# The turns of two score steps in one run of every second slot

## The chip, the cores and the metric

The kernel runs on one core of one Trainium2 chip. The metric is the device time of one launch in microseconds (us). The kernel before takes 1454.48 us (median of three runs, 1454.06 to 1455.24). Engines are named as in the profile: PE is TensorE (its weight loads are PEld), DVE is VectorE, ACT is ScalarE, POOL is GpSimd, SP issues the weight loads from memory.

## What is computed

Two residual layers over x (512 tokens, width 1024). Each layer normalises x, projects it by `w_in`, runs two attention mixers of 16 heads of 64 columns over the 512 tokens, gates, projects, merges and adds. What matters here are the mixers. The sparse one (NSA) has two softmax branches per head over full causal keys (the selection takes all eight blocks, the window is as long as the sequence) and a small compressed branch with 31 keys; the other (FoX) has one causal softmax per head with a forgetting bias:

```python
s = jnp.einsum('bqhd,bkhd->bhqk', qc, k).astype(jnp.float32) * scale
s = s + Fq[..., None] - F[:, :, None, :]
p = masked_softmax(s, mask)
return jnp.einsum('bhqk,bkhd->bqhd', p.astype(v.dtype), v)
```

So per layer there are 16 x 3 causal attentions of 512 x 512, each in four query tiles of 128 rows, whose key widths are 128, 256, 384 and 512.

## The kernel before

Every matmul is done in two parts for precision: an fp32 operand is split into an upper part (rounded, by ACT) and a lower part (the rest, by DVE).

A layer's attentions run in eight **cycles** (function `cycles`), one per pair of heads, each followed on all engines by a `body(cycle)` of its own. A cycle has 24 **steps**: 16 for NSA (two heads, two branches, four query tiles, in the order of `NSA_ORDER`, whose widths are 256, 128, 128, 384, 512, 256, 384, 512 columns, twice) and 8 for FoX (128, 256, 384, 512, twice). The first and the last cycle of a layer have variants; the six between are alike, and are called steady below.

A step passes through the engines:

1. PE makes its scores (`score_step`, L1874 and L1876), in two PSUM banks;
2. DVE takes the row maximum and copies the scores out (`max_step`, L1400, with a read of the accumulator);
3. ACT exponentiates and sums (`exp_step`, L936, with a read of the accumulator);
4. DVE inverts the sum (`invert_step`, L1407), POOL scales the row (`scale_step`, L727 and L730);
5. PE turns the probabilities, one transpose per 128 columns, into one of two PSUM banks (`turn_step`, L1889);
6. ACT copies out the upper part (`hi_step`, L945), then DVE the lower part (`lo_step`, L1412), into a buffer for an attention of that parity;
7. when an attention's four steps are done, PE multiplies with the values (`value_step` L1914, and the last key tile later, `value_narrow` L1922), into one bank, `o_pair`. After a head's last attention ACT copies that bank's lower half (`lower_half`, L950) and DVE adds the upper half (`head_output`, L1419).

The work is written out as **slots**, and the order in a slot is the order in which an engine's queue has it. In slot s of a cycle:

- PE: turns of step s-2 (LAG_TURN = 2), scores of step s+1, then a piece of the projections of the next pair (`unit_piece`, L1814), then what is in `extra` (values of a step s-4 that ends an attention, the compressed branch). The turn of step n waits until the lower part of step n-2 is out of its bank.
- ACT: exponent of step s, upper part of step s-2, then its list `todo` (splits of weights `w_hi` L807, roundings of q, k and v, `lower_half`).
- DVE: reciprocal of step s-1, maximum of step s, lower part of step s-3 (LAG_PT = 3, `lo_step` waits for that step's upper part), then its `todo` (`w_lo` L1217, copies of the projections, `head_output`).
- POOL: scaling of step s-1, then its `todo`.

How many of the 144 unit matmuls of a cycle stand in a slot is set by `Plan`: it gives each slot the costs of scores, turns and values (`busy`) and spreads the units over what is left (`spread`). The slots in which a unit begins and ends (`plan.begin`, `plan.end`) place the splits and copies on ACT and DVE.

Of the kernel before, what the change touches and what calls it, by code (L numbers as in the profile page):

```python
# [51 lines left out]
CYCLE_STEPS = 24  # L52
# [5 lines left out]

GAINS, PLACES = (DEPTH + 1) * KT, 2 * DEPTH * CJ
LAG_SCALE, LAG_TURN, LAG_PT, LAG_PV = 1, 2, 3, 4  # L60
PT_COLS = 3 * 384 + T


# [10 lines left out]
    return cum  # L74


NSA_ORDER = [(0, 1), (0, 0), (1, 0), (0, 2), (0, 3), (1, 1), (1, 2), (1, 3)]
SCORE_COST = {(0, 0): 1.0, (1, 0): 0.0}


class Plan:


    def __init__(self, last=False):
        self.last = last
        self.slots = CYCLE_STEPS + (LAG_PV if last else 0)
        busy = [0.0] * self.slots
        for s in range(self.slots):
            for lag, cost in ((-1, self.score_cost), (LAG_TURN, self.turn_cost), (LAG_PV, self.value_cost)):
                if not last or s - lag < CYCLE_STEPS:  # L90
                    busy[s] += cost((s - lag) % CYCLE_STEPS)
        for s, cost in ((1, 2.0), (5, 2.0), (9, 1.0), (17, 1.0)):
            busy[s] += cost
        self.cum = spread(24 * 6, busy)
        self.begin, self.end = {}, []
        for u in range(6):
            first = next(s for s in range(self.slots) if self.cum[s] > 24 * u)
            self.begin.setdefault(first, []).append(u)
            self.end.append(next(s for s in range(self.slots) if self.cum[s] >= 24 * u + 24))
# [88 lines left out]
def bass_trunk(nc, x, norm_g, w_in, b_forget, pe_k, w1_k, w2_k, pe_v, w1_v, w2_v, w_nsa, w_fox,  # L188
               w_out, final_g, rope_c, rope_s, out):
    ctx = ExitStack()  # L190
    with ctx:
# [429 lines left out]
        def _(pool):  # L621
# [66 lines left out]
            def gate_output(pair):  # L688

                pool.wait_ge(o_read, 2 * pair.r + 3)  # L690
                apart(pool)
                pool.wait_ge(z_done, pair.r + 2)
                apart(pool)
                y = y_all[0 if pair.nsa else 1][:, bass.ds(pair.i, 1), :]
                pool.tensor_tensor(y, y, z_silu[:, pair.b:pair.b + 1, :], ALU.mult).then_inc(y_mul, 1)
# [37 lines left out]
            def body(cycle):  # L733
                plan, l, i = cycle.plan, cycle.l, cycle.i
                todo = {}

                def at(slot, what):
                    todo.setdefault(slot, []).append(what)

                at(0, lambda: bias_of(cycle.fox))  # L740
                at(2, lambda: compressed_shift(cycle.nsa.m))
                at(4, lambda: compressed_scale(cycle.nsa.m, i))
                if not cycle.first:
                    at(10, lambda: gate_output(Pair(False, l, i - 1, cycle.g)))
                at(CYCLE_STEPS + 1 if cycle.last else 16 + LAG_PV + 2, lambda: gate_output(cycle.nsa))
                if cycle.last:
                    at(CYCLE_STEPS + LAG_PV, lambda: gate_output(cycle.fox))
                else:
                    at(plan.end[2] + 4, lambda: q_sin(l * 10 + 3 + i))
                    at(plan.end[2] + 5, lambda: q_sum(l * 10 + 3 + i))  # L750
                for s in range(max([plan.slots] + [k + 1 for k in todo])):
                    if s < plan.slots and s - LAG_SCALE < CYCLE_STEPS and cycle.step(s - LAG_SCALE):
                        scale_step(*cycle.step(s - LAG_SCALE))
                    for what in todo.get(s, []):
                        what()
# [43 lines left out]
        def _(act):  # L799
# [100 lines left out]
            def body(cycle):  # L900
# [3 lines left out]
                def at(slot, what):  # L904
                    todo.setdefault(slot, []).append(what)
# [34 lines left out]
                def hi_step(pair, s):  # L940
                    a, qt = pair.at(s)
                    act.wait_ge(s_turned, pair.s0 + s + 1)
                    if pair.starts(s) and not (cycle.first and pair.nsa and a < 2):
                        act.wait_ge(pv_mm, pair.a0 + a - 1)
                    act.activation(pt_tiles(pt_hi, a, qt), turned_tiles(s, qt), ACT.Copy)\  # L945
                        .then_inc(pt_hi_done, 1)

                def lower_half(pair, h):
                    act.wait_ge(pv_mm, pair.a0 + pair.steps // QT // 2 * (h + 1))
                    act.activation(o_low[:, h, :], o_pair[HD:2 * HD, :], ACT.Copy, scale=0.5).then_inc(o_low_done, 1)  # L950

                if not cycle.first:
                    before = Pair(False, l, i - 1, cycle.g)
                    at(0, lambda: lower_half(before, 0))
                    at(LAG_PV, lambda: lower_half(before, 1))
                at(8 + LAG_PV, lambda: lower_half(nsa, 0))
                at(16 + LAG_PV, lambda: lower_half(nsa, 1))
                if cycle.last:
                    at(CYCLE_STEPS, lambda: lower_half(fox, 0))
                    at(CYCLE_STEPS + LAG_PV, lambda: lower_half(fox, 1))  # L960
                    at(plan.end[4] + 3, lambda: gate_tanh(l, 0, 0))

# [18 lines left out]
                for s in range(max([plan.slots] + [k + 1 for k in todo])):  # L981
                    if s < CYCLE_STEPS:
                        exp_step(*cycle.step(s))
                    if s < plan.slots and s - LAG_TURN < CYCLE_STEPS and cycle.step(s - LAG_TURN):
                        hi_step(*cycle.step(s - LAG_TURN))
                    for what in todo.get(s, []):
                        what()

# [224 lines left out]
        def _(dve):  # L1213
# [130 lines left out]
            def body(cycle):  # L1344
# [76 lines left out]

                if not cycle.first:
                    before = Pair(False, l, i - 1, cycle.g)
                    at(1, lambda: head_output(before, 0))
                    at(LAG_PV + 2, lambda: head_output(before, 1))
                at(8 + LAG_PV + 2, lambda: head_output(nsa, 0))
                at(16 + LAG_PV + 1, lambda: head_output(nsa, 1))
                if cycle.last:
                    at(CYCLE_STEPS + 1, lambda: head_output(fox, 0))
                    at(CYCLE_STEPS + LAG_PV, lambda: head_output(fox, 1))  # L1430

                m = nsa.m
# [348 lines left out]
        def _(pe):  # L1781
# [58 lines left out]
            def body(cycle):  # L1840
                plan, l, i, nsa, fox = cycle.plan, cycle.l, cycle.i, cycle.nsa, cycle.fox
                extra = {}
# [104 lines left out]
                        pe.wait_ge(cmp_pt_lo, nsa.m + 1)  # L1947
                    pe.matmul(o_pair[:, :], vcb[:, nsa.g, h, :], pc_t[:, :], start=False, stop=False)  # L1948

                for slot, what in ((1, cmp_scores), (5, cmp_turn), (9, lambda: cmp_values(0)),  # L1950
                                   (17, lambda: cmp_values(1))):
                    extra.setdefault(slot, []).insert(0, what)
                for s in range(plan.slots):

                    now = cycle.step(s - LAG_PV)
                    if s - LAG_PV < CYCLE_STEPS and now and now[0].ends(now[1]):
                        extra.setdefault(s, []).append(lambda now=now: value_step(now[0], now[0].at(now[1])[0]))

                def ended_at(s):

                    now = cycle.step(s - 1 - LAG_PV) if s - 1 - LAG_PV < CYCLE_STEPS else None
                    return (now[0], now[0].at(now[1])[0]) if now and now[0].ends(now[1]) else None

                if cycle.first:
                    score_step(nsa, 0)
# [2 lines left out]
                for s in range(max([plan.slots] + [k + 1 for k in extra])):  # L1968
                    scored = cycle.step(s + 1) if s < CYCLE_STEPS else None
                    narrow = scored and not scored[0].nsa and scored[0].starts(scored[1])  # L1970
                    if s < plan.slots and s - LAG_TURN < CYCLE_STEPS and cycle.step(s - LAG_TURN):
                        turn_step(*cycle.step(s - LAG_TURN), scored=scored if narrow else None, ended=ended_at(s))
                    elif s < plan.slots and ended_at(s):
                        value_narrow(*ended_at(s), 0)
                        value_narrow(*ended_at(s), 1)
                    if scored and not narrow:
                        score_step(*scored)
                    want = plan.cum[s] if s < plan.slots else done
                    while done < want:
                        u = done // 24  # L1980
                        stop = min(want, 24 * u + 24)
                        unit_piece(done - 24 * u, stop - 24 * u, *cycle.unit(u), free=bank_read(cycle, u))
                        done = stop
                    for what in extra.get(s, []):
                        what()
                if cycle.last:
                    value_narrow(*ended_at(plan.slots), 0)
                    value_narrow(*ended_at(plan.slots), 1)

            def run_in(n):  # L1990
                for _ in range(n):
# [232 lines left out]
```

## Time and profile before

| | |
|---|---|
| Time, median of three runs | 1454.48 us |
| Span of the profiled execution | 1452.2 us |
| PE busy | 1443.0 us (99%) |
| DVE busy | 1050.6 us (72%) |
| ACT busy | 915.4 us (63%) |
| POOL busy | 469.1 us (32%) |
| Chain that ended last | PE 98%, DVE 1% |
| Most of the chain | PE L1814 69%, PE L1889 8%, PE L1914 7% |

The profile was taken in one execution, whose own total time is not given; its span of 1452.2 us lies 2.3 us below the median. Busy shares are of the whole span; the span holds the layers' attention cycles (two stretches of 450 us) and other stages (projections, merge, output) between them.

### The profile page before, as it was taken

Reading aid. Unit: us, or ns where it says so; the run is one execution under the profiler, and the core shown is the slowest. Engines: PE = TensorE matmul, PEld = TensorE weight load, DVE = VectorE, ACT = ScalarE, POOL = GpSimd, SP = SyncE. Lnnn points to the kernel's source line nnn. Section 1 sums busy time; section 2 is a strip of 40 time slices with the busy share of each in tenths; the row PEclk is TensorE's granted clock in tenths of the full one; section 3 lists DMA queues with packets and bytes.
Section 4 is the critical chain, followed back from the end, with each engine's and each line's share of the span. In section 5 each row is a group of like instructions: output and inputs, shape, how many; then the busy total and the mean of one; then the engine's idle time right before and its main releaser. Section 6 shows DMA issues by size and latency. Waiting matters only on the chain.

```text
span 1452.2 us, 24707 instructions
## 1 busy us (share of the span) xinstructions
PE 1443.0 (99%) x7550; PEld 1223.2 (84%) x7550; DVE 1050.6 (72%) x2422; ACT 915.4 (63%) x1904; POOL 469.1 (32%) x578
## 2 busy tenths in 40 slices
PE   9999999999999999999999999999999999999998
PEld 7888888888888888888888888888888888888887
DVE  6888888888888864444578888888888887643444
ACT  6677777777877752223365877877877876522234
POOL 2435535445445310000023345445445453000000
PEclk9999999999999999999999999999999999999999
DMA  9221222222222143333453222222222212433332
GB/s 285 75 69 49 59 58 58 59 56 51 55 58 59 46 144 97 91 101 93 110 183 83 57 54 59 58 59 59 59 58 55 61 44 59 145 95 102 92 102 91
DMA packets 213890, 117.97 MB, mean 81 GB/s; under 512 B 9304, under 2 KB 212272, under 8 KB 213296
## 3 DMA queue, kind: packets, MB, share of 16 engines
q1 hardware_dynamic: 211408, 107.49, 27.2%
q0 software_dynamic: 1728, 8.66, 1.6%
q8 instruction: 39, 0.64, 0.2%
q10 hardware_dynamic: 672, 0.83, 0.2%
q14 instruction: 43, 0.35, 0.1%
HBM read 110.54 MB, written 6.42 MB: 81 GB/s over the span
## 4 chain that ended last, share of the span: by engine, by line
PE 98%; DVE 1%; issue 0%; ACT 0%; POOL 0%; DVEq 0%; POOLq 0%; ACTq 0%
PE acc L1814 69%; PE turned L1889 8%; PE o_pair L1914 7%; PE scores L1874 4%; PE scores L1876 4%; PE turned L2056 1%; PE misc L1933 1%; PE o_pair L1922 1%; PE scores L1814 1%; PE misc L1837 1%; PE o_pair L1948 1%; PE acc L2171 0%; PE o_pair L2171 0%; PE o_pair L2073 0%; PE scores L1992 0%
## 5 line engine op out<-in xcount | busy, mean ns | idle before, releaser
L1814 PE MATMUL acc<-u_hi,w_hi 128*128 128x512 f32 x1096 | 433.4, 395 | 0.0
L1814 PE MATMUL acc<-u_lo,w_hi 128*128 128x512 f32 x1096 | 430.9, 393 | 0.0
L1814 PE MATMUL acc<-u_hi,w_lo 128*128 128x512 f32 x1096 | 428.3, 393 | 0.0
L936 ACT ACTIVATE prob<-prob,row_max 128x384 f32<-128x384 f32 (+3 forms) x384 | 215.5, 561 | 143.2 <-DVE row_max L1400 140.8
L1217 DVE TENSOR_TENSOR w_lo<-w_raw,w_hi 128x1024 fp32r<-128x1024 f32 x184 | 230.7, 1254 | 83.1 <-ACT w_hi L807 82.4
L730 POOL TENSOR_SCALAR prob<-prob,row_inv,gates 128x256 f32<-128x256 f32 (+3 forms) x256 | 168.2, 657 | 302.8 <-DVE row_inv L1407 302.0
L807 ACT ACTIVATE w_hi<-w_raw 128x1024 fp32r<-128x1024 f32 x184 | 193.6, 1053 | 87.7 <-PE acc L1814 82.9
L1814 PEld LDWEIGHTS acc<-u_hi,w_hi 128*128 128x128 f32 x1096 | 206.4, 188 | 39.1 <-issue 0.2
L1814 PEld LDWEIGHTS acc<-u_lo,w_hi 128*128 128x128 f32 x1096 | 206.0, 188 | 37.0 <-issue 0.2
L1814 PEld LDWEIGHTS acc<-u_hi,w_lo 128*128 128x128 f32 x1096 | 206.4, 188 | 36.3
L1400 DVE CUSTOM_DVE_ANT_0 prob<-scores,causal 128x384 f32<-128x384 f32 (+3 forms) x384 | 185.7, 484 | 45.0 <-PE scores L1876 34.1
L945 ACT ACTIVATE pt_hi<-turned 128x384 fp32r<-128x384 f32 (+3 forms) x384 | 164.2, 428 | 52.1 <-PE turned L1889 46.8
L1412 DVE TENSOR_TENSOR pt_lo<-turned,pt_hi 128x384 fp32r<-128x384 f32 (+3 forms) x384 | 186.5, 486 | 4.6 <-ACT pt_hi L945 2.4
L1889 PE MATMUL turned<-ident,prob 128*128 128x128 f32 x960 | 177.4, 276 | 1.2 <-DVE pt_lo L1412 0.8
L727 POOL TENSOR_SCALAR prob<-prob,row_inv 128x128 f32<-128x128 f32 (+3 forms) x128 | 144.8, 1136 | 89.8 <-DVE row_inv L1407 89.8
L1889 PEld LDWEIGHTS turned<-ident,prob 128*128 128x128 f32 x960 | 120.2, 141 | 28.8 <-POOL prob L730 5.3
L1814 PE MATMUL acc<-yt_hi,w_lo 128*128 128x512 f32 x256 | 99.6, 389 | 0.0
L1814 PE MATMUL acc<-yt_hi,w_hi 128*128 128x512 f32 x256 | 99.6, 389 | 0.0
L1814 PE MATMUL acc<-yt_lo,w_hi 128*128 128x512 f32 x256 | 99.6, 389 | 0.0
L1407 DVE RECIPROCAL row_inv<-row_sum 128x1 f32<-128x1 f32 x384 | 61.3, 160 | 51.4 <-ACT prob L936 43.1
L1874 PE MATMUL scores<-kk_hi,q_nsa 128*128 128x256 f32 (+2 forms) x224 | 91.2, 407 | 0.0
L897 ACT ACTIVATE m_th<-m_th 128x512 f32<-128x512 f32 x32 | 20.2, 631 | 87.1 <-DVE m_th L1260 87.1
(276 smaller groups left out, 2346.1 us busy)
## 6 DMA issues: line engine op xcount, KB each, us to landing
w_raw<-in_w_in_dram SPq DMA_DIRECT2D x140, 512.0 KB, 3.7
w_raw<-in_w_proj_nsa_dram SPq DMA_DIRECT2D x16, 512.0 KB, 3.6
w_raw<-in_w_proj_fox_dram SPq DMA_DIRECT2D x16, 512.0 KB, 3.6
w_raw<-in_w_out_dram SPq DMA_DIRECT2D x16, 512.0 KB, 3.7
x_scratch<-xT POOLq DMA_DIRECT2D x2, 2048.0 KB, 9.2
xT<-x_scratch POOLq DMA_DIRECT2D x2, 2048.0 KB, 8.3
x_nat<-in_x_dram SPq DMA_DIRECT2D x4, 512.0 KB, 6.7
c_w<-in_cmp_w_k_dram SPq DMA_DIRECT2D x4, 512.0 KB, 6.1
```

What stands on the lines that cost most here:

```text
L727: ins = pool.tensor_scalar(p, p, row_inv[:, ring:ring + 1], None, ALU.mult)
L730: ins = pool.tensor_scalar(p, p, row_inv[:, ring:ring + 1], gate, ALU.mult, ALU.mult)
L807: act.activation(w_hi[:, par, :, 0:width], w_raw[:, par, :, 0:width], ACT.Copy).then_inc(w_hi_done, 1)
L936: act.activation(prob[:, ring, 0:width], prob[:, ring, 0:width], ACT.Exp, bias=row_max[:, ring:ring + 1], scale=-1.0, accum_out=row_sum[:, ...
L945: act.activation(pt_tiles(pt_hi, a, qt), turned_tiles(s, qt), ACT.Copy)\
L1217: dve.tensor_tensor(w_lo[:, par, :, 0:width], w_raw[:, par, :, 0:width], w_hi[:, par, :, 0:width], ALU.subtract).then_inc(w_lo_done, 1)
L1400: dve.tensor_tensor_reduce(prob[:, ring, 0:width], scores[bank][:, first:first + width], causal[:, T - width:T], -SCALE, BIG, ALU.add, ALU ...
L1412: dve.tensor_tensor(pt_tiles(pt_lo, a, qt), turned_tiles(s, qt), pt_tiles(pt_hi, a, qt), ALU.subtract).then_inc(pt_lo_done, 1)
L1814: ins = pe.matmul((bank or acc[par])[0:width, :], own_w, rhs, start=(n == 0), stop=(n == 23))
L1874: pe.matmul(to, q_hi, k_hi, start=True, stop=False)
L1889: ins = pe.transpose(turned[s % 2][:, P * kt:P * kt + P], prob[:, s % SM_RING, P * kt:P * kt + P], ident[:, :])
L1914: pe.matmul(o_pair[:, q0:T], v, pt[:, a % 2, 384 * kt + q0:384 * kt + T], start=first and (kt, m) == (0, 0), stop=False)
```

## The change

`both(s, lag)` names, for every slot in which `s - lag` is odd, the two steps s-lag-1 and s-lag, and none for the other slots. PE turns the steps s-3 and s-2 one after the other in each odd slot and none in the even ones; ACT makes the two upper parts in that slot, after the exponent of step s; DVE's order stays as it was, a lower part of step s-3 in each slot. The value steps come in odd slots, their narrow ends two slots after them. `lower_half` comes one slot later, `head_output` in part one slot later, the compressed values one slot later. `Plan` counts the costs where they now stand.

```diff
+LAG_NARROW = LAG_PV + 2
+def both(s, lag):
+    return (lag + 1, lag) if (s - lag) % 2 else ()
...
-            for lag, cost in ((-1, self.score_cost), (LAG_TURN, self.turn_cost), (LAG_PV, self.value_cost)):
-                if not last or s - lag < CYCLE_STEPS:
-                    busy[s] += cost((s - lag) % CYCLE_STEPS)
-        for s, cost in ((1, 2.0), (5, 2.0), (9, 1.0), (17, 1.0)):
+            for lags, cost in (((-1,), self.score_cost), (both(s, LAG_TURN), self.turn_cost),
+                               (both(s, LAG_PV), self.value_cost)):
+                for lag in lags:
+                    if not last or s - lag < CYCLE_STEPS:
+                        busy[s] += cost((s - lag) % CYCLE_STEPS)
+        for s, cost in ((1, 2.0), (5, 2.0), (10, 1.0), (18, 1.0)):
...
 # POOL
-                at(CYCLE_STEPS + 1 if cycle.last else 16 + LAG_PV + 2, lambda: gate_output(cycle.nsa))
+                at(CYCLE_STEPS + 1 if cycle.last else 16 + LAG_PV + 3, lambda: gate_output(cycle.nsa))
 # ACT
-                    at(0, lambda: lower_half(before, 0))
-                    at(LAG_PV, lambda: lower_half(before, 1))
-                at(8 + LAG_PV, lambda: lower_half(nsa, 0))
-                at(16 + LAG_PV, lambda: lower_half(nsa, 1))
+                    at(1, lambda: lower_half(before, 0))
+                    at(LAG_PV + 1, lambda: lower_half(before, 1))
+                at(8 + LAG_PV + 1, lambda: lower_half(nsa, 0))
+                at(16 + LAG_PV + 1, lambda: lower_half(nsa, 1))
...
-                    if s < plan.slots and s - LAG_TURN < CYCLE_STEPS and cycle.step(s - LAG_TURN):
-                        hi_step(*cycle.step(s - LAG_TURN))
+                    for lag in both(s, LAG_TURN):
+                        if s < plan.slots and s - lag < CYCLE_STEPS and cycle.step(s - lag):
+                            hi_step(*cycle.step(s - lag))
 # DVE
-                    at(1, lambda: head_output(before, 0))
+                    at(2, lambda: head_output(before, 0))
-                at(16 + LAG_PV + 1, lambda: head_output(nsa, 1))
+                at(16 + LAG_PV + 2, lambda: head_output(nsa, 1))
...
 # PE
-                for slot, what in ((1, cmp_scores), (5, cmp_turn), (9, lambda: cmp_values(0)),
-                                   (17, lambda: cmp_values(1))):
+                for slot, what in ((1, cmp_scores), (5, cmp_turn), (10, lambda: cmp_values(0)),
+                                   (18, lambda: cmp_values(1))):
+                def ending(s, lag):
+                    for n in (s - each for each in both(s, lag)):
+                        now = cycle.step(n) if n < CYCLE_STEPS else None
+                        if now and now[0].ends(now[1]):
+                            return now[0], now[0].at(now[1])[0]
+                    return None
                 for s in range(plan.slots):
-                    now = cycle.step(s - LAG_PV)
-                    if s - LAG_PV < CYCLE_STEPS and now and now[0].ends(now[1]):
-                        extra.setdefault(s, []).append(lambda now=now: value_step(now[0], now[0].at(now[1])[0]))
+                    if ending(s, LAG_PV):
+                        extra.setdefault(s, []).append(lambda now=ending(s, LAG_PV): value_step(*now))
                 def ended_at(s):
+                    return ending(s, LAG_NARROW)
...
-                    if s < plan.slots and s - LAG_TURN < CYCLE_STEPS and cycle.step(s - LAG_TURN):
-                        turn_step(*cycle.step(s - LAG_TURN), scored=scored if narrow else None, ended=ended_at(s))
-                    elif s < plan.slots and ended_at(s):
+                    turns = [cycle.step(s - lag) for lag in both(s, LAG_TURN) if s < plan.slots and s - lag < CYCLE_STEPS]
+                    turns = [step for step in turns if step]
+                    for n, step in enumerate(turns):
+                        turn_step(*step, scored=scored if narrow and n == 0 else None, ended=ended_at(s) if n == 0 else None)
+                    if not turns and s < plan.slots and ended_at(s):
                         value_narrow(*ended_at(s), 0)
                         value_narrow(*ended_at(s), 1)
```

## Rows read from the trace of the kernel before

**Rows 1.** Stretches, busy us (instructions) per engine: first, six steady, last cycle
```profile
65.10:117.80 52.70, 52.69 (x290) 44.84 (x289) 46.06 (x127) 38.63 (x90) 19.58 (x28) 1.00 0.23 62
117.80:454.50 336.70, 336.70 (x1873) 288.73 (x1872) 281.20 (x769) 260.79 (x601) 163.27 (x198) 1.00 0.22 57
454.50:504.70 50.20, 49.61 (x279) 41.95 (x278) 41.39 (x123) 36.21 (x90) 24.72 (x31) 1.00 0.20 54
```

**Rows 2.** DVE's waits in the six steady cycles: total us, times, longest
```profile
DVE row_inv L1407 <- ACT prob L936: 15.4, 42, 0.7
DVE prob L1400 <- PE scores L1876: 14.6, 24, 1.0
DVE w_lo L1217 <- ACT w_hi L807: 8.3, 24, 0.6
DVE q_fox L1307 <- ACT q_fox L856: 4.4, 6, 0.7
```

**Rows 3.** DVE in order of time: start us, us, operation; slot 12 of a cycle
```profile
320.00 0.69 DVE L1400 CUSTOM_DVE_ANT_0 prob<-scores,causal 128x512 f32<-128x512 f32 x1
320.62 0.08 DVE L1400 DVE_READ_ACCUMULATOR2_ANT row_max<- 128x1 f32 x1
320.62 0.28 DVE L1412 TENSOR_TENSOR pt_lo<-turned,pt_hi 128x128 fp32r<-128x128 f32 x1
321.58 0.17 DVE L1407 RECIPROCAL row_inv<-row_sum 128x1 f32<-128x1 f32 x1 [0.68 <-ACT prob L936]
```

**Rows 4.** ACT in order of time, the same slot
```profile
320.74 0.72 ACT L936 ACTIVATE prob<-prob,row_max 128x512 f32<-128x512 f32 x1 [0.84 <-DVE row_max L1400]
321.46 0.26 ACT L945 ACTIVATE pt_hi<-turned 128x128 fp32r<-128x128 f32 x1
321.62 1.05 ACT L807 ACTIVATE w_hi<-w_raw 128x1024 fp32r<-128x1024 f32 x1
```

**Rows 5.** Exponents and upper parts in steady cycles by width: busy us, mean ns | idle before
```profile
L936 ACT ACTIVATE prob<-prob,row_max 128x512 f32<-128x512 f32 x36 | 26.1, 724 | 11.5 <-DVE row_max L1400 11.2
L936 ACT ACTIVATE prob<-prob,row_max 128x384 f32<-128x384 f32 x36 | 22.2, 617 | 26.6 <-DVE row_max L1400 26.5
L945 ACT ACTIVATE pt_hi<-turned 128x512 fp32r<-128x512 f32 x37 | 21.8, 589 | 1.1
L936 ACT ACTIVATE prob<-prob,row_max 128x256 f32<-128x256 f32 x36 | 18.1, 504 | 5.3 <-DVE row_max L1400 5.2
L945 ACT ACTIVATE pt_hi<-turned 128x384 fp32r<-128x384 f32 x36 | 17.5, 485 | 8.2 <-PE turned L1889 7.9
L936 ACT ACTIVATE prob<-prob,row_max 128x128 f32<-128x128 f32 x36 | 14.4, 401 | 9.0 <-DVE row_max L1400 8.6
L945 ACT ACTIVATE pt_hi<-turned 128x256 fp32r<-128x256 f32 x36 | 13.4, 373 | 6.3 <-PE turned L1889 6.2
L945 ACT ACTIVATE pt_hi<-turned 128x128 fp32r<-128x128 f32 x36 | 9.6, 267 | 4.8 <-PE turned L1889 4.0
```

**Rows 6.** DVE in order of time, slot 7 of the same cycle
```profile
307.96 0.08 DVE L1400 DVE_READ_ACCUMULATOR2_ANT row_max<- 128x1 f32 x1
```

**Rows 7.** ACT in order of time, end of slot 6 and start of slot 7
```profile
309.37 0.77 ACT L975 ACTIVATE pc_t<-misc 64x256 fp32r<-64x256 f32 x2
310.17 0.72 ACT L936 ACTIVATE prob<-prob,row_max 128x512 f32<-128x512 f32 x1
```

**Rows 8.** PE in order of time, a run of three turns and what follows
```profile
304.06 0.49 PE L1889 MATMUL turned<-ident,prob 128*128 128x128 f32 x3
304.30 0.42 PE L1874 MATMUL scores<-kk_hi,q_nsa 128*128 128x384 f32 x1
304.56 0.33 PE L1876 MATMUL scores<-kk_lo,q_nsa 128*128 128x384 f32 x1
304.73 0.40 PE L1814 MATMUL acc<-u_hi,w_lo 128*128 128x512 f32 x1
```

**Rows 9.** PE in the last 12.2 us: length, busy us (instructions), granted clock, DMA
```profile
1440.00:1452.20 12.20, 6.76 (x57) 0.87 0.43 173
```

More of the change, by code:

```diff
@@ L953, in body @@
                     before = Pair(False, l, i - 1, cycle.g)
-                    at(0, lambda: lower_half(before, 0))
-                    at(LAG_PV, lambda: lower_half(before, 1))
-                at(8 + LAG_PV, lambda: lower_half(nsa, 0))
-                at(16 + LAG_PV, lambda: lower_half(nsa, 1))
+                    at(1, lambda: lower_half(before, 0))
+                    at(LAG_PV + 1, lambda: lower_half(before, 1))
+                at(8 + LAG_PV + 1, lambda: lower_half(nsa, 0))
+                at(16 + LAG_PV + 1, lambda: lower_half(nsa, 1))
                 if cycle.last:
-                    at(CYCLE_STEPS, lambda: lower_half(fox, 0))
+                    at(CYCLE_STEPS + 1, lambda: lower_half(fox, 0))
                     at(CYCLE_STEPS + LAG_PV, lambda: lower_half(fox, 1))
@@ L1423, in body @@
                     before = Pair(False, l, i - 1, cycle.g)
-                    at(1, lambda: head_output(before, 0))
+                    at(2, lambda: head_output(before, 0))
                     at(LAG_PV + 2, lambda: head_output(before, 1))
                 at(8 + LAG_PV + 2, lambda: head_output(nsa, 0))
-                at(16 + LAG_PV + 1, lambda: head_output(nsa, 1))
+                at(16 + LAG_PV + 2, lambda: head_output(nsa, 1))
                 if cycle.last:
-                    at(CYCLE_STEPS + 1, lambda: head_output(fox, 0))
+                    at(CYCLE_STEPS + 2, lambda: head_output(fox, 0))
                     at(CYCLE_STEPS + LAG_PV, lambda: head_output(fox, 1))
@@ L1948, in cmp_values @@
                     pe.matmul(o_pair[:, :], vcb[:, nsa.g, h, :], pc_t[:, :], start=False, stop=False)
-                for slot, what in ((1, cmp_scores), (5, cmp_turn), (9, lambda: cmp_values(0)),
-                                   (17, lambda: cmp_values(1))):
+                for slot, what in ((1, cmp_scores), (5, cmp_turn), (10, lambda: cmp_values(0)),
+                                   (18, lambda: cmp_values(1))):
                     extra.setdefault(slot, []).insert(0, what)
+                def ending(s, lag):
[4 more added lines that the diff above has]
+                    return None
                 for s in range(plan.slots):
-                    now = cycle.step(s - LAG_PV)
-                    if s - LAG_PV < CYCLE_STEPS and now and now[0].ends(now[1]):
-                        extra.setdefault(s, []).append(lambda now=now: value_step(now[0], now[0].at(now[1])[0]))
+                    if ending(s, LAG_PV):
+                        extra.setdefault(s, []).append(lambda now=ending(s, LAG_PV): value_step(*now))
                 def ended_at(s):
-                    now = cycle.step(s - 1 - LAG_PV) if s - 1 - LAG_PV < CYCLE_STEPS else None
-                    return (now[0], now[0].at(now[1])[0]) if now and now[0].ends(now[1]) else None
+                    return ending(s, LAG_NARROW)
                 if cycle.first:
@@ L1986, in body @@
                 if cycle.last:
-                    value_narrow(*ended_at(plan.slots), 0)
-                    value_narrow(*ended_at(plan.slots), 1)
+                    value_narrow(fox, 1, 0)
+                    value_narrow(fox, 1, 1)
             def run_in(n):
```

## The prediction

> **What bounds the kernel now.** I read the stretches first. In the attention cycles PE is busy all the time: 336.7 of 336.7 us in the six steady cycles of a layer, 56.1 us each; in the first cycle 52.69 of 52.7, in the last 49.61 of 50.2 [rows 1]. The granted clock is 1.00 there, so PE is at its upper level (2.4 GHz), and a microsecond taken from PE's order would be a microsecond off the time, as long as nobody else is late. The second number in those rows is DVE: 281.2 us in six cycles, 46.9 us of each 56.1. It has 9.25 us a cycle to spare, 0.77 us per pair of slots, and every one of its orders stands in one queue, so a wait at its head holds everything behind.
>
> Next the waits of DVE. They are small: 15.4 us in six cycles for the exponent (before the reciprocal), 14.6 us for PE's scores, 8.3 us for `w_hi`, 4.4 us for the rounding of q [rows 2]. No wait before the lower part is among the large ones, as its upper part was made a slot earlier. That DVE waits for scores 24 times shows that it keeps up with PE and follows it closely.
>
> Then the order in time of one slot. DVE starts the maximum at 320.00 and the lower part at 320.62, without a pause [rows 3]. ACT starts the exponent of that maximum at 320.74 and the next upper part at 321.46 [rows 4]. The lower part in this slot belongs to an older step.
>
> **What the change does to DVE.** It leaves the number of instructions on every engine as it is, and moves them. The step that decides stands on no line of the diff's DVE part: DVE still makes the lower part of step s-3 in slot s, directly after the maximum of step s. In odd slots the upper part of s-3 is now made in the same slot s, on ACT's queue behind the exponent of step s, and that exponent needs the maximum which DVE has only just made. So in each odd slot DVE stands still for maximum → exponent → upper part. Behind it wait the reciprocal of s, the next maximum, and all copies of that slot; for these wait POOL's scaling, the exponent, PE's next scores and turns.
>
> The wait, from rows. The exponent starts 0.12 us after the point where the lower part could start (320.74 against 320.62) [rows 3, 4]. The exponents of the twelve odd steps of a cycle are 2 of 128 columns, 4 of 256, 2 of 384, 4 of 512 (order of the steps): (2 x 0.401 + 4 x 0.504 + 2 x 0.617 + 4 x 0.724) / 12 = 0.58 us [rows 5]; the upper part starts as the exponent ends (320.74 + 0.72 = 321.46) [rows 4]. The upper parts of the even steps are 4 of 128, 2 of 256, 4 of 384, 2 of 512: (4 x 0.267 + 2 x 0.373 + 4 x 0.485 + 2 x 0.589) / 12 = 0.41 us [rows 5]. A semaphore from one engine to the other takes 0.04 us (the read of the maximum ends at 320.70, ACT starts at 320.74) [rows 3, 4]. Sum 0.12 + 0.58 + 0.41 + 0.04 = 1.15 us, twelve times a cycle: 13.8 us. That is more than the 9.25 us to spare.
>
> To this comes ACT's lateness. The exponent of an odd step waits for what ACT does in the even slot before. Slot 7 shows the worst: the maximum is out at 307.96 + 0.08 = 308.04, but the exponent starts at 310.17, 2.1 us later, behind the rounding of q and the copies `pc_t` [rows 6, 7]. Today that delays nobody. An upper part of 384 to 512 columns (0.5 us, rows 5) leaves the slot before it, so 1.5 us stay. `w_hi` (1.05 us, rows 4) stands in the even slots 0, 4 and 12, and the value and q roundings in 18; setting ACT's 0.7 (maximum) + 0.5 to 0.7 (exponent) + 1.05 against DVE's work in the same slot I get 0.3, 0.5, 0.3 and 0.2 us. `lower_half` moves from the even to the odd slots behind the upper parts, where it delays nothing. Together 2.8 us a cycle; the bounds are 0 and, if nothing leaves slot 6 and each `w_hi` counts whole, 2.1 + 3 x 1.05 = 5.3. The value is nearer the middle as each was set against DVE's own work in that slot.
>
> What goes in exchange: the odd slots' reciprocals no longer wait (the exponent is done before the lower part is), nor `w_lo` and the q rests in odd slots, nor DVE for scores, because PE is now the one that runs ahead. Of the waits of [rows 2] I keep 0.7 us a cycle, for reciprocals in even slots (bounds 0 and half of the first row plus all of the second, 1.3 + 2.4 = 3.7).
>
> A steady cycle is then DVE's: 46.9 + 13.8 + 2.8 + 0.7 = 64.2 us, 8.1 more than 56.1. The first cycle has 11 such slots and less lateness: 46.1 + 12.7 + 1.7 + 2.0 (today's waits in it that stay) = 62.5, 9.8 more than 52.7. The last: 41.4 + 13.8 + 2.3 + 1.2 = 58.7, 8.5 more than 50.2. Over two layers 12 x 8.1 + 2 x 9.8 + 2 x 8.5 = 134 us. The profiled span of 1452.2 becomes 1586; with the 2.3 us between span and median, 1588 us.
>
> **The other parts.** Turns on PE: three turns take 304.30 - 304.06 = 0.24 us, and the score matmul behind them 0.26 where its like takes 0.17, so 0.33 in all, 0.11 per turn [rows 8]. Counted so, a run has no price of its own, and two runs made one save nothing; at most the stretched matmul (0.09 us) goes 12 times a cycle, 1.1 us, and that would be hidden now, since PE has 8 us to spare. Below: a run of up to 0.88 us could delay the scores behind it, hidden likewise. I take 0. Value steps in odd slots, narrow ends two slots later, compressed values later: same matmuls; the narrow end stands before the turn of the attention that reuses its buffer, and `head_output` still comes at least a slot before the value step that needs the bank. I take 0, at most the 0.5 us of one `lower_half` once or twice a cycle, inside the range's upper end. The unit plan of a steady cycle begins and ends its units in the same slots as before; in the last cycle three of them shift by one slot: 0. POOL's `gate_output` one slot later: it is idle most of the time, 163 of 337 us busy [rows 1]: 0. POOL and SP issue their DMAs in the same place.
>
> The clock: it is 1.00 in the cycles, and falls only in the last stretch, where PE is busy 6.76 of 12.2 us (0.87 on average there) [rows 1, 9]. By the Trainium skill, TensorE: Matmul & The Clock Gate, section "HAM oscillation — how this bites in real kernels", a PE whose idle gaps grow long is set back to half its clock, which would speak against any change that makes PE wait. By that rule too short pauses leave the clock alone, and I expect PE's 8 us a cycle in pieces around 1 us.
>
> **The rivals.** (A) Only the bare waits: ACT is never late and every other wait of DVE vanishes. Cycles of 60.7, 58.8 and 55.2 us: 12 x 4.6 + 2 x 6.1 + 2 x 5.0 = 77 us more, 1531 us. For it: DVE's slower pace gives ACT more time. Against: slot 7. (B) The waits for PE and for the exponents stay beside the new ones, 3.0 us a cycle more than in my sum: 48 us, 1636 us. For it: the matmuls are bunched in odd slots. Against: PE has 8 us of slack. (C) Clock: waits drop PE to its lower level (1.2 GHz) half the time in the cycles: its 56.1 us become 84, 20 more than DVE's 64: 16 x 20 = 320, 1906 us. (D) Faster: PE stays the bound because DVE's wait is under 0.77 us per odd slot, and PE is spared the stretched matmul behind every second run: 12 x 0.09 x 16 = 17 us, 1437 us. It decides at 9.25 us of new waiting a cycle. For it: PE is the whole chain today. Against: exponent and upper part of the mean size alone are 0.99 us. That the turns are not joined is excluded by the order written out.
>
> **How the numbers follow.** Forecast 0.55, A 0.19, B 0.18, C 0.03, D 0.05 (0.04 of it faster by over 0.2%, 0.01 within 0.2%, which is about what a measurement can tell from no change). So faster 0.04, same 0.01, slower 0.95. Predicted is 1588 us. The range of 8 in 10 goes from A's 1531 to a little above B's, 1531 to 1642.
>
> **What would show it.** In the profile after: the lower part (L1412) gets a wait for ACT's upper part (L945) of some 16 us a steady cycle, in 12 of 24 slots, where it had none; DVE's busy time a cycle stays at 47 us and a steady cycle is about 64 us; the chain moves from PE to DVE and ACT in the cycles; PE waits, about 8 us a cycle, for DVE; the clock stays at 1.00; stages outside the cycles keep their lengths. Wrong would be: steady cycles of 56 us, or waits before the lower part under 9 us a cycle; or longer cycles whose DVE has no such wait.

## The result and the profile after

The changed kernel takes 1568.42 us (median of 5 runs, 1567.7 to 1568.85), the kernel before 1454.48 us (5 runs). The ratio is 1.0783, 95% interval 1.0771 to 1.0795: 114 us slower, where 134 were forecast.

Stretches of the changed kernel: first cycle, six steady cycles and last cycle of the first layer, then the stage between the layers' cycles. Columns are start and end, length, busy us (instructions) of PE, PEld, DVE, ACT, POOL, the granted clock, DMA share, GB/s. They answer to [rows 1].

```profile
65.10:125.80 60.70, 57.09 (x305) 48.14 (x304) 46.43 (x129) 38.14 (x90) 19.83 (x28) 1.00 0.22 57
125.80:507.60 381.80, 353.98 (x1875) 300.77 (x1874) 280.09 (x769) 254.35 (x600) 156.79 (x198) 0.96 0.20 50
507.60:561.90 54.30, 48.13 (x266) 40.30 (x265) 40.33 (x118) 36.37 (x89) 22.17 (x30) 1.00 0.19 50
561.90:837.40 275.50, 274.42 (x1262) 227.88 (x1261) 151.58 (x181) 112.92 (x155) 26.67 (x25) 1.00 0.40 114
```

The reader should see three things. A steady cycle has gone from 56.1 to 63.6 us (381.8 / 6). DVE's busy time in it is what it was, 46.7 us against 46.9 [rows 1]. And PE, which was never idle in a steady cycle, is idle 28 us in six. The first cycle is 8.0 us longer, the last 4.1; the stage between the layers' cycles has kept its length (275.5 us, 275.4 before).

Who DVE waited for in the same six cycles (total us, times, longest); it answers to [rows 2]:

```profile
DVE pt_lo L1421 <- ACT pt_hi L953: 91.5, 72, 3.1
DVE row_inv L1416 <- ACT prob L944: 5.1, 12, 0.7
```

The four waits of before have become one large and one small one. The large one comes 72 times, which is 12 a cycle, one for each odd slot, 15.25 us a cycle. The waits for PE's scores are gone, so PE no longer sets the pace.

The worst slot is number 7. The chain of waits of the changed kernel there, from the end of slot 6 on, in order of time (start us, length us, what; some pieces left out at the dots):

```profile
273.10 0.46 DVE prob L1409
...
274.12 0.19 ACT prob L944
274.31 0.95 ACT q_fox L864
275.27 1.06 ACT q_fox L864
...
276.36 0.38 ACT pc_t L983
...
277.15 0.82 ACT prob L944 x2
277.99 0.61 ACT pt_hi L953
278.62 0.70 DVE pt_lo L1421
279.46 0.53 PE turned L1898 x3
280.05 0.69 DVE q_fox L1316
280.76 0.42 DVE pc_t L1463
...
281.65 0.17 DVE row_inv L1416
...
281.99 0.78 POOL prob L738
282.81 1.11 PE turned L1898 x4
```

It passes from DVE's maximum of slot 6 to ACT. There it runs through the rounding of q (`q_fox`) and the copies `pc_t`, which stand in the queue ahead of slot 7, and only then through the exponent and the upper part of slot 7. From there it goes back to DVE's lower part, over three turns of PE and DVE's own copies of that slot to the reciprocal, and by POOL's scaling to PE's next turns. None of PE's matmuls of the units stands on it here. DVE and PE at the same place, in order of time:

```profile
275.46 0.08 DVE L1409 DVE_READ_ACCUMULATOR2_ANT row_max<- 128x1 f32 x1
278.62 0.69 DVE L1421 TENSOR_TENSOR pt_lo<-turned,pt_hi 128x512 fp32r<-128x512 f32 x1 [3.08 <-ACT pt_hi L953]
279.46 0.52 PE L1898 MATMUL turned<-ident,prob 128*128 128x128 f32 x3 [0.59 <-DVE pt_lo L1421]
282.81 1.11 PE L1898 MATMUL turned<-ident,prob 128*128 128x128 f32 x4 [2.83 <-POOL prob L738]
283.58 0.78 PE L1823 MATMUL acc<-u_lo,w_hi 128*128 128x512 f32 x1
```

### The profile page after: what moved, and what is told of

The parts are those of the page before. It is cut to its first block, busy times and chain, and to the rows that moved or that the text cites. A ratio compares the mean times of both kernels' runs of the same rounds, so it can differ in the third digit from the quotient of the medians.

```text
span 1567.1 us, 24697 instructions
## 1 busy us (share of the span) xinstructions
PE 1482.5 (95%) x7550; PEld 1249.8 (80%) x7550; DVE 1045.2 (67%) x2422; ACT 900.8 (57%) x1904; POOL 455.0 (29%) x578
## 4 chain that ended last, share of the span: by engine, by line
PE 58%; DVE 19%; ACT 10%; issue 10%; POOL 2%; DVEq 1%; ACTq 0%; POOLq 0%
PE acc L1823 42%; DVE prob L1409 4%; PE o_pair L1923 4%; PE turned L1898 3%; ACT prob L944 3%; ACT pt_hi L953 3%; DVE pt_lo L1421 3%; DVE w_lo L1226 3%; ACT q_fox L864 2%; PE scores L1883 2%; PE scores L1885 2%; DVE row_inv L1416 2%; POOL prob L735 1%; PE turned L2073 1%; DVE qk_raw L1269 1%
## 5 line engine op out<-in xcount | busy, mean ns | idle before, releaser
L738 POOL TENSOR_SCALAR prob<-prob,row_inv,gates 128x256 f32<-128x256 f32 (+3 forms) x256 | 155.6, 608 | 416.1 <-DVE row_inv L1416 415.3
L1898 PE MATMUL turned<-ident,prob 128*128 128x128 f32 x960 | 166.5, 285 | 76.6 <-POOL prob L738 40.9
L1898 PEld LDWEIGHTS turned<-ident,prob 128*128 128x128 f32 x960 | 111.3, 143 | 110.8 <-POOL prob L738 58.4
L735 POOL TENSOR_SCALAR prob<-prob,row_inv 128x128 f32<-128x128 f32 (+3 forms) x128 | 139.4, 1090 | 116.4 <-DVE row_inv L1416 116.2
L953 ACT ACTIVATE pt_hi<-turned 128x384 fp32r<-128x384 f32 (+3 forms) x384 | 144.6, 426 | 6.6 <-PE turned L1898 5.1
L1883 PE MATMUL scores<-kk_hi,q_nsa 128*128 128x256 f32 (+2 forms) x224 | 86.4, 386 | 0.0
L1885 PE MATMUL scores<-kk_lo,q_nsa 128*128 128x256 f32 (+2 forms) x224 | 75.1, 336 | 0.0
L1923 PE MATMUL o_pair<-pt_hi,v_pair 128*128 128x512 f32 (+2 forms) x192 | 71.8, 374 | 0.0
```

Source lines behind the costliest of these rows:

```text
L735: ins = pool.tensor_scalar(p, p, row_inv[:, ring:ring + 1], None, ALU.mult)
L738: ins = pool.tensor_scalar(p, p, row_inv[:, ring:ring + 1], gate, ALU.mult, ALU.mult)
L1883: pe.matmul(to, q_hi, k_hi, start=True, stop=False)
L1898: ins = pe.transpose(turned[s % 2][:, P * kt:P * kt + P], prob[:, s % SM_RING, P * kt:P * kt + P], ident[:, :])
L1923: pe.matmul(o_pair[:, q0:T], v, pt[:, a % 2, 384 * kt + q0:384 * kt + T], start=first and (kt, m) == (0, 0), stop=False)
```

## The experiments

Each kernel ran beside the kernel before on the same chip. Before took 1454.89 us beside `lower_in_pairs`, `upper_first`, `upper_pairs_alone` and `q_fox_later`, and 1454.63 us beside the other four, so times of the two groups can be compared with each other and with the changed kernel's 1568.42 us. The expectations name three theories of the loss. Theory 1: DVE waits in the odd slot for its own maximum, the exponent and the upper part. Theory 2: the joined turns and values on PE, with POOL's scaling and the clock. Theory 3, for one run: ACT's lateness only moves to another slot.

**Lower parts in pairs too** (`lower_in_pairs`). The changed kernel, with DVE making both lower parts in the even slot after their upper parts.

```diff
-                    if step(LAG_PT):
-                        lo_step(*step(LAG_PT))
+                    for lag in both(s, LAG_PT):
+                        if step(lag):
+                            lo_step(*step(lag))
```

> The changed kernel with one line more: DVE makes both lower parts in the even slot after their upper parts (none in odd slots). Theory 1, DVE's own wait for maximum, exponent and upper part in the odd slot is the loss: the 15.2 us a steady cycle before the lower part vanish, a steady cycle goes from 63.5 back to 56 us, 1454 us (1450 to 1460), clock 1.00. Theory 2, the joined turns and values on PE (bunched work, turns waiting for POOL's scaling, the clock's drops) are the loss: PE still waits for POOL and the time stays above 1540 us.

Measured: 1453.77 us, ratio 0.9992 (0.9982 to 1.0002). Its six steady cycles, and DVE's largest waits in them:

```profile
123.50:459.70 336.20, 336.20 (x1873) 291.12 (x1872) 278.83 (x769) 259.18 (x600) 161.63 (x199) 1.00 0.21 57
```
```profile
DVE row_inv L1416 <- ACT prob L944: 23.9, 48, 0.9
DVE prob L1409 <- PE scores L1886: 8.0, 19, 0.5
```

PE is busy 336.2 of 336.2 us again, and waits for the lower part are no longer among DVE's. One reordering on DVE, the lower parts of the even steps one slot later, gives the whole loss back, while turns, values, unit plan and ACT stay as changed. Joined turns and values on PE are excluded as the cause. The clock is back at 1.00 too, so this run does not part the clock from the waits; that is done by cycles of equal length at 0.97 and 1.00 (under the clock, below). The run also measures the joined turns with the pairs on ACT and DVE around them: no difference from the kernel before that can be told (1.1 us less, inside the interval).

**Upper part before the exponent** (`upper_first`). ACT's odd slots in the order upper part of s-3, exponent of s, upper part of s-2.

```diff
-                    if s < CYCLE_STEPS:
-                        exp_step(*cycle.step(s))
-                    for lag in both(s, LAG_TURN):
-                        if s < plan.slots and s - lag < CYCLE_STEPS and cycle.step(s - lag):
-                            hi_step(*cycle.step(s - lag))
+                    for lag in (LAG_TURN + 1, None, LAG_TURN):
+                        if lag is None:
+                            if s < CYCLE_STEPS:
+                                exp_step(*cycle.step(s))
+                        elif lag in both(s, LAG_TURN) and s < plan.slots and s - lag < CYCLE_STEPS and cycle.step(s - lag):
+                            hi_step(*cycle.step(s - lag))
```

> The changed kernel with ACT's odd slots in another order: upper part of step s-3, then the exponent of s, then the upper part of s-2. It takes the exponent (0.58 us) out of DVE's wait. Theory 1: at least 0.58 us of the 1.27 us go in each of 12 odd slots, 7 us a cycle or more, and the time falls under 1480 us, if the turn of s-3 is early enough; the exponent may then wait for the turn. Theory 2: over 1540 us.

Measured: 1490.64 us, 1.0246 (1.0229 to 1.0264). DVE's waits in six steady cycles:

```profile
DVE pt_lo L1422 <- ACT pt_hi L953: 51.3, 50, 2.2
DVE row_inv L1417 <- ACT prob L944: 10.6, 31, 0.7
```

The wait before the lower part falls from 15.25 to 8.55 us a cycle, by 6.7, near the 12 x 0.58 = 7.0 of the exponents. The steady cycle falls less, from 63.6 to 58.7, by 4.9, since DVE's other waits and pauses grow by 1.8 (table below). So the time missed the 1480 of the expectation by 11. In the wait that is left stand the upper part itself, ACT's lateness and, new, ACT waiting for PE's turn (24.0 us in 315 us of the cycles, 0.8 us in six cycles of the changed kernel).

**ACT's part of the change alone** (`upper_pairs_alone`). The kernel before, with only the upper parts paired.

```diff
-                    if s < plan.slots and s - LAG_TURN < CYCLE_STEPS and cycle.step(s - LAG_TURN):
-                        hi_step(*cycle.step(s - LAG_TURN))
+                    for lag in (LAG_TURN + 1, LAG_TURN) if (s - LAG_TURN) % 2 else ():
+                        if s < plan.slots and s - lag < CYCLE_STEPS and cycle.step(s - lag):
+                            hi_step(*cycle.step(s - lag))
```

> The kernel before with one edit: ACT makes both upper parts in the odd slots, as the change does. PE's order, the unit plan and all other lists are those of before. Theory 1: DVE waits as in the changed kernel, 15 us a cycle, and the time is 1555 to 1575 us. Theory 2: without joined turns and values nothing is lost, 1454 us.

Measured: 1609.26 us, 1.1062 (1.1044 to 1.1081). PE's order is that of before, and the loss is there, even 41 us larger than in the changed kernel. So the pairs on ACT are enough to cause it, and another part of the change softens it. The waits show which slots: those before the lower part are 107.3 us in six cycles (91.5 in the changed kernel), and by slot the excess lies in 1, 5, 13 and 21 (1.89 against 1.12 us in slot 1, 1.71 against 0.94 in slot 5). Ahead of these slots ACT has `lower_half` here, and not in the changed kernel.

**The same with `lower_half` one slot later** (`upper_pairs_half_later`).

```diff
-                    at(0, lambda: lower_half(before, 0))
-                    at(LAG_PV, lambda: lower_half(before, 1))
-                at(8 + LAG_PV, lambda: lower_half(nsa, 0))
-                at(16 + LAG_PV, lambda: lower_half(nsa, 1))
+                    at(1, lambda: lower_half(before, 0))
+                    at(LAG_PV + 1, lambda: lower_half(before, 1))
+                at(8 + LAG_PV + 1, lambda: lower_half(nsa, 0))
+                at(16 + LAG_PV + 1, lambda: lower_half(nsa, 1))
...
```

What is left out at the dots moves `head_output` on DVE and `gate_output` on POOL one slot later too, and `lower_half` of the last cycle.

> The kernel before with both upper parts in odd slots (as in upper_pairs_alone) and also lower_half, head_output and gate_output in the slots of the changed kernel; PE's order and the unit plan of before. If the 41 us between upper_pairs_alone (1609) and the changed kernel (1568) are the copy lower_half (0.6 us) standing in four even slots ahead of the exponents of odd steps, this run is at 1568 us (1563 to 1573). If they are owed to PE's joined turns, it stays at 1609 us.

Measured: 1573.4 us, 1.0816, 0.4 us above the range of the expectation. Steady cycles are 63.7 us, those of the changed kernel, with the same waits (91.4 us):

```profile
131.20:513.20 382.00, 347.39 (x1874) 290.55 (x1873) 280.16 (x769) 256.38 (x601) 157.26 (x199) 0.99 0.18 50
```
```profile
DVE pt_lo L1413 <- ACT pt_hi L945: 91.4, 72, 3.1
```

So four copies of 0.6 us ahead of an odd slot's exponent cost 2.5 us a steady cycle, all on the path, and 36 us in the whole kernel. Of the 5 us by which it stays above the changed kernel 3.5 are in the last cycles (56.6 in both layers against 54.3 and 55.4 us); their cause was not sought.

**A dose on ACT** (`act_dose`). Two small copies before the upper part of s-3.

```diff
+        dose = sb("dose", [P, 2, 104])
...
+                    if twice:
+                        for n in range(2):
+                            act.activation(dose[:, n, :], turned[s % 2][:, 0:104], ACT.Copy)
...
-                            hi_step(*cycle.step(s - lag))
+                            hi_step(*cycle.step(s - lag), twice=lag > LAG_TURN)
```

> The changed kernel with two small copies more on ACT (104 columns of the turned bank into a place nobody reads) before the upper part of step s-3 in each odd slot: some 0.35 us more between maximum and lower part, 12 times a cycle. Theory 1: the whole dose lands on the path, 12 x 16 x 0.35 = 67 us, 1635 us. If the cycles were bound elsewhere (PE, POOL, the clock): ACT is idle 21 us of 63.5 and hides it, 1568 us.

Measured: 1620.73 us, 1.1143. DVE's wait before the lower part:

```profile
DVE pt_lo L1425 <- ACT pt_hi L957: 111.8, 72, 3.4
```

111.8 against 91.5 us in six cycles is 3.4 us a cycle more, 0.28 per odd slot. The dose was smaller than the 0.35 expected: ACT's busy time grew by 0.29 us per odd slot (from 254.3 to 275.4 us in six cycles). 16 x 3.4 = 54 us; measured against the changed kernel, 52 us. ACT is idle a third of the time and hides none of it.

**The rounding of q one slot later** (`q_fox_later`).

```diff
-                    at(plan.end[0] + 2, lambda: qf_round([(qk_raw_done, qk + 1), (s_mm, nsa.s0 + 1)]))
+                    at(plan.end[0] + 3, lambda: qf_round([(qk_raw_done, qk + 1), (s_mm, nsa.s0 + 1)]))
-                    at(plan.end[0] + 3, lambda: qf_rest(parts))
+                    at(plan.end[0] + 4, lambda: qf_rest(parts))
-                at(7 if cycle.last else 6, cmp_copy)
+                at(7, cmp_copy)
-                at(8 if cycle.last else 7, cmp_rest)
+                at(8, cmp_rest)
```

> The changed kernel with the rounding of q for FoX and the copies pc_t on ACT in slot 7 instead of 6, and what DVE makes of them in slot 8 instead of 7 (steady cycles). Theory 1, with ACT's lateness a term of its own: the wait before the lower part in slot 7 falls from 3.1 to 1.5 us, 12 steady cycles gain 1.5 us each, 1550 us; the long wait of PE there, and the clock's drops, go. Theory 2, the drops of the clock themselves cost: as they go too, more than 30 us is gained. Theory 3: the lateness only moves to slot 8 or 9, 1568 us.

Measured: 1559.48 us, 1.0722. Half of theory 1's gain. The waits before the lower part went from 91.5 to 81.9 us, longest 1.5 instead of 3.1:

```profile
DVE pt_lo L1421 <- ACT pt_hi L953: 81.9, 72, 1.5
DVE q_fox L1316 <- ACT q_fox L864: 2.7, 6, 0.5
```

Slot 7's wait halved as expected, 1.6 us a cycle less, but 0.45 us came back in slot 8 before DVE's own q rest and 0.14 in slot 9. The lateness is a term of its own, and partly movable; theory 3 does not fit. On theory 2 the run says little, since the clock's falls did not go as expected: ten were left of thirteen in the cycles of both layers, with PE's longest wait in a steady cycle still 1.7 us.

**Pairs for one kind of step only** (`fox_in_pairs`, `nsa_in_pairs`). The condition is `not now[0].nsa` in the first and `now[0].nsa` in the second.

```diff
-                    if step(LAG_PT):
-                        lo_step(*step(LAG_PT))
+                    for lag in (LAG_PT + 1, LAG_PT):
+                        now = step(lag)
+                        late = now and now[1] % 2 == 0 and (not now[0].nsa)
+                        if now and late == (lag > LAG_PT):
+                            lo_step(*now)
```

> Lower parts in pairs in the even slots for the 8 FoX steps only; the 8 waits of NSA's even steps stay (10.8 us a steady cycle, of 15.2). Theory 1: DVE needs 46.7 + 10.8 + 1.2 = 58.7 us a cycle, 2.6 over PE's 56.1, so 1454 + 16 x 2.6 = 1495 us. A loss in proportion to the waits left (10.8 of 15.2) would give 1454 + 0.71 x 114 = 1535 us.

Measured: 1527.9 us, 1.0504.

```profile
128.40:493.20 364.80, 346.76 (x1874) 296.69 (x1873) 279.69 (x769) 256.77 (x600) 158.76 (x199) 0.98 0.19 52
```
```profile
DVE pt_lo L1421 <- ACT pt_hi L953: 67.8, 48, 3.1
```

> Lower parts in pairs for the 16 NSA steps only; FoX's 4 waits stay (4.4 us a steady cycle). Theory 1, with DVE's slack of about 9 us as the point from which waits count: 46.7 + 4.4 + some 3 us of other waits is under 56.1, 1454 us (up to 1460). In proportion to the waits left (4.4 of 15.2): 1454 + 0.29 x 114 = 1487 us.

Measured: 1474.37 us, 1.0137 (1.0121 to 1.0154).

```profile
126.20:470.00 343.80, 338.28 (x1876) 290.55 (x1874) 278.61 (x769) 255.47 (x600) 161.38 (x199) 1.00 0.21 56
```
```profile
DVE pt_lo L1421 <- ACT pt_hi L953: 27.8, 25, 1.3
DVE row_inv L1416 <- ACT prob L944: 21.1, 36, 0.9
DVE q_fox L1316 <- ACT q_fox L864: 3.7, 6, 0.6
DVE w_lo L1226 <- ACT w_hi L815: 3.5, 12, 0.4
DVE kf_lo L1328 <- ACT kf_hi L877: 3.0, 6, 0.6
```

Both missed theory 1's figures, by 33 and 20 us, and the losses in proportion to the waits left (1535 and 1487 us) were nearer, 7 and 13 us too high. The misses have one form: I had left too little for DVE's other waits. In `nsa_in_pairs` they are 31.3 us in six cycles, 5.2 a cycle, with 1.1 of pauses, not 3 in all. In `fox_in_pairs` the waits before the lower part were 11.3, not 10.8, with 2.9 of others, not 1.2. The table takes a steady cycle apart by DVE's time (us, from stretches and waits divided by six; "rest" is the length less the three before it, so the rows add up by construction):

| kernel | length | DVE busy | wait for upper part | other waits named | rest |
|---|---|---|---|---|---|
| changed | 63.6 | 46.7 | 15.3 | 0.9 | 0.8 |
| act_dose | 66.7 | 46.3 | 18.6 | 0.9 | 0.9 |
| fox_in_pairs | 60.8 | 46.6 | 11.3 | 1.6 | 1.3 |
| upper_first | 58.7 | 46.6 | 8.6 | 1.9 | 1.6 |
| nsa_in_pairs | 57.3 | 46.4 | 4.6 | 5.2 | 1.1 |

What the table shows is that busy time stays and the rest is small, and that the waits trade: from `fox_in_pairs` to `nsa_in_pairs` the wait for the upper part falls by 6.7 us, the other waits rise by 3.6, and the cycle falls by 3.5. So the loss follows neither a fixed slack nor a proportion. Who sets the pace is seen elsewhere: in all five DVE's waits for PE's scores are 0.2 us or less in six cycles (`fox_in_pairs` has 1.6 us for PE's turns); in the two whose cycle is about 56.1 us (before, `lower_in_pairs`) they are 14.6 and 8.0 us.

## Why the prediction was right

The direction, the mechanism and the range held; the size was 20 us too high.

*DVE's wait for its own maximum, the exponent and the upper part.* Shown. It is there in 12 of 24 slots, it goes with one line on DVE (1453.77 us), it shrinks by the exponents when these are taken out of it, and it grows with the dose. The bare wait was put at 1.15 us; slots 9, 11, 17, 19, 21, where ACT is not late, show 0.94 to 1.16 (mean 1.05).

*ACT's lateness, 2.8 us a cycle.* Right in kind: slot 7's wait is 3.08 us, of which 1.6 is lateness, where 1.5 was forecast. Behind `w_hi`, in slots 1, 5 and 13, it was less than the 0.3, 0.5 and 0.3 forecast. Slot 5 of one cycle, DVE and then ACT:

```profile
269.91 0.08 DVE L1409 DVE_READ_ACCUMULATOR2_ANT row_max<- 128x1 f32 x1
269.28 1.05 ACT L815 ACTIVATE w_hi<-w_raw 128x1024 fp32r<-128x1024 f32 x1
270.23 0.50 ACT L944 ACTIVATE prob<-prob,row_max 128x256 f32<-128x256 f32 x1
```

The exponent starts 0.24 us after the maximum is read, where it starts 0.035 us after it when ACT is waiting. In the mean of the twelve steady cycles the exponents of slots 1, 5 and 13 are 0.2, 0.1 and 0.1 us late by this reckoning, that of slot 19 not at all. Together with slot 7 that is 2.0 us a cycle, which leaves 13.2 for the bare waits (13.8 forecast). All waits together are 15.3 us where 16.6 were forecast.

*A steady cycle of 64.2 us.* Measured 63.6: 7.5 longer, not 8.1. *The first cycle:* 8.0 longer, not 9.8. *The last:* 4.1 longer in the first layer, where 8.5 were forecast. That is the term sized worst: I counted its odd slots as twelve waits with 2.3 us of lateness (16.1 us in all), but the stretch ends before the twelfth wait and holds 11 waits of 13.0 us in all. Behind it nothing is added: from the start of the last exponent of layer one to the first of layer two it is 275.5 us, and 275.4 before. The sum by measured terms: 2 x 8.0 + 12 x 7.5 + 2 x 4.6 (the two last cycles are 4.1 and 5.2 longer) = 115 us; the span grew from 1452.2 to 1567.1.

*What went in exchange.* As said: no waits for scores, none for `w_lo`, reciprocals 0.9 us a cycle (0.7 forecast). PE is idle 4.6 us a steady cycle, not 8: its busy time grew from 56.1 to 59.0 us.

*Joined turns cost and save nothing.* Shown by `lower_in_pairs` within its interval (2.6 us faster to 0.3 us slower), while PE was the bound; a saving of the 17 us of rival D is excluded.

*Moving `lower_half` "delays nothing".* Half right: it delays nothing where it is now; I did not see that it would have cost 2.5 us a cycle had it stayed. Moving it took 36 us off where only the pairs on ACT were changed (1609.26 to 1573.4 us).

*The clock.* I expected it at 1.00, with PE's pauses around 1 us; it was 0.96 in the first layer's steady cycles (stretch above), and one pause a cycle was 2.83 us. It explains about 1 us of the 114, an estimate from three cycles that are some 0.2 to 0.6 us longer than the others. Two steady cycles of the changed kernel, the first with the clock low for longer:

```profile
189.30:253.20 63.90, 59.18 (x313) 50.42 (x312) 46.72 (x129) 42.47 (x100) 26.13 (x33) 0.95 0.19 49
253.20:316.50 63.30, 58.77 (x314) 49.85 (x313) 46.55 (x129) 42.28 (x100) 26.13 (x33) 0.97 0.20 51
```

The two cycles of the layer at 0.95 took 63.9 and 64.1 us, with a wait of 1.44 and 1.64 us in slot 11, the four at 0.97 took 63.3 to 63.5, with 1.04. The second layer has one more such cycle. The shorter falls cost nothing here: neighbouring cycles of `upper_pairs_half_later` are 63.7 us at 0.97 and at 1.00. Rival C's cost did not come, because the clock was low for a small part of a cycle and PE had time to spare.

## What to carry to other kernels

Where a queue runs in order, the distance between a wait and the work that ends it is a count of queue positions, not of steps: before moving work on one engine to a later slot, look at every consumer whose slot stays, and ask whether the producer now stands behind something that needs what this very consumer has just made. Here DVE's lower part came to wait for an upper part behind an exponent that needed DVE's own latest maximum. Moving the consumer by the same distance (one reordering on DVE) kept the kernel at its old time. And an engine at 84% busy, as DVE was in the cycles, is no cover for waits in its own chain: add its busy time and the waits that cannot overlap, and compare that sum with the bound. The sum was near for the whole change (134 us forecast, 114 measured) and poor for half of it (`fox_in_pairs`, `nsa_in_pairs`), where other waits grew as the large one shrank.

## What the runs showed of the hardware

The clock fell during or just after a short wait of PE that repeats once a cycle. In the changed kernel PE does three turns between two waits, 0.59 and 2.83 us (PE's rows above). Stretches around it:

```profile
279.00:282.00 3.00, 0.52 (x3) 0.31 (x3) 2.85 (x7) 0.81 (x1) 0.01 (x1) 1.00 0.00 0
282.10:285.40 3.30, 2.59 (x9) 2.30 (x10) 2.60 (x8) 1.27 (x5) 1.21 (x2) 0.57 0.09 5
285.50:288.00 2.50, 2.50 (x13) 2.21 (x12) 2.37 (x6) 2.44 (x7) 1.56 (x2) 0.90 0.69 200
```

PE is busy 0.52 of 3.00 us; then the granted clock is at its lower level (1.2 GHz) for most of the next stretch, and a unit matmul takes 0.78 us where it took 0.39 to 0.40. In `nsa_in_pairs`, where PE's longest wait in the steady cycles is 1.0 us, the clock stays at 1.00 in them.

Between these lengths the same wait may or may not bring a fall, and a fall can cost more than in the changed kernel. `upper_first` has one wait of 1.8 to 1.9 us in every steady cycle, and the clock fell in one cycle of six in each layer. Two cycles of it, and PE's turns behind that wait in each:

```profile
243.70:303.80 60.10, 58.19 (x315) 49.97 (x314) 46.49 (x129) 42.99 (x102) 27.16 (x35) 0.97 0.20 54
303.80:362.30 58.50, 56.45 (x314) 48.43 (x313) 46.66 (x128) 42.56 (x102) 26.91 (x34) 1.00 0.20 55
```
```profile
266.32 0.66 PE L1899 MATMUL turned<-ident,prob 128*128 128x128 f32 x4 [1.88 <-POOL prob L738]
326.31 0.66 PE L1899 MATMUL turned<-ident,prob 128*128 128x128 f32 x4 [1.88 <-POOL prob L738]
```

The wait is the same 1.88 us in both. The cycle with the fall is 1.6 us longer than its neighbour, and so it is in the second layer (60.1 against 58.3 and 58.4 us). That PE has less to spare there, 2.1 us a cycle against 4.6 in the changed kernel, fits this, but was not tested by itself. What decides in which cycle the clock falls no run here shows.
